# Selecting token rows over 128 partitions, and for one expert first in each layer's first group

## The reference, cut to what matters

```python
def hier_moe(x, wg, bg, we, be, w_gate_up, w_down):
    ...
    gsel = jnp.argmax(lg, axis=-1)                 # one of 4 groups per token
    ...
    topv, topi = lax.top_k(le_sel, MOE_TOP_K)      # 2 of the group's 4 experts
    wt = jax.nn.softmax(topv, axis=-1) * p_sel
    ...
    hu = jnp.einsum('td,edf->tef', xt, w_gate_up)  # 2048 -> 2*512 per expert
    hg, hv = jnp.split(hu, 2, axis=-1)
    act = jax.nn.silu(hg) * hv * gates[..., None].astype(x.dtype)
    out = jnp.einsum('tef,efd->td', act, w_down)   # 512 -> 2048
```

## Time and profile before

| | |
|---|---|
| median of 3 runs | 1442.11 us (1439.29 to 1442.18) |
| the profiled execution's own time | 1440.58 us |
| its span in the profile | 1438.5 us |
| TensorE matmul busy | 1354.8 us (94%) |
| TensorE weight load busy | 753.8 us (52%) |
| VectorE / ScalarE busy | 517.0 / 370.5 us |
| DMA | 489.03 MB, mean 340 GB/s |
| layer 0, first selection | 387.74 us into the span |
| layer 1, first selection | 941.09 us into the span |

### The profile page before, as it was taken

How to read it: one execution, slowest core, us unless ns; L and a number is a source line. 1 busy time by engine, 2 the same in 40 slices (tenths; PEclk the granted TensorE clock), 3 DMA queues, 4 the chain that set the end, 5 groups by cost and what they waited for, 6 DMA issues and landing times.

```text
span 1438.5 us, 20688 instructions
## 1 busy us (share of the span) xinstructions
PE 1354.8 (94%) x8992; PEld 753.8 (52%) x8992; DVE 517.0 (36%) x1068; ACT 370.5 (26%) x576; POOL 30.8 (2%) x40
## 2 busy tenths in 40 slices
PE   8999999999899999999899998899999899889985
PEld 8999999999643433343243226653243243224321
DVE  6877887743442122022004016633042013103303
ACT  5667666442310120030012004410021012002001
POOL 0000000000000000000000000000000000000000
PEclk9999999999899999999999999999999999999998
DMA  9776452944599999999999988689999999999993
GB/s 296 241 211 191 138 186 77 293 163 171 201 390 405 428 413 428 426 427 428 428 427 428 426 343 309 245 300 354 427 426 428 427 427 427 428 427 427 426 428 128
DMA packets 94759, 489.03 MB, mean 340 GB/s; under 512 B 8409, under 2 KB 64665, under 8 KB 67577
## 3 DMA queue, kind: packets, MB, share of 16 engines
q1 hardware_dynamic: 89536, 468.61, 82.0%
q10 hardware_dynamic: 2458, 10.27, 2.1%
q0 software_dynamic: 2672, 8.82, 1.6%
HBM read 481.95 MB, written 16.04 MB: 346 GB/s over the span
## 4 chain that ended last, share of the span: by engine, by line
PE 70%; DMA 25%; DVE 2%; ACT 1%; issue 1%; ACTq 0%; DVEq 0%; POOL 0%; SPq 0%; POOLq 0%
DMA ring<-in_moe_w_down 23%; PE ps L1325 19%; PE ps L1304 17%; PE ps L1071 5%; PE ps L1073 5%; PE ps L1072 5%; PE ps L1223 5%; PE ps L1159 2%; PE ps L1388 2%; PE ps L1160 2%; PE ps L1161 2%; PE ps L1247 1%; DMA ring<-in_lru_w_in 1%; ACT xtok L676 1%; DMA xtok<-x_rows,src_now 1%
## 5 line engine op out<-in xcount | busy, mean ns | idle before, releaser
L1304 PE MATMUL ps<-ring,xsel 128*64 128x512 f32 x2016 | 451.2, 596 | 30.1 <-DMA ring<-in_moe_w_gate_up 29.1
L1325 PE MATMUL ps<-ring,work 128*32 128x512 f32 x3072 | 342.9, 594 | 16.6 <-DMA ring<-in_moe_w_down 16.6
L1304 PEld LDWEIGHTS ps<-ring,xsel 128*64 128x64 f32 x2016 | 137.5, 137 | 316.7 <-issue 258.3
L1325 PEld LDWEIGHTS ps<-ring,work 128*32 128x32 f32 x3072 | 93.5, 110 | 234.2 <-issue 210.1
L1922 DVE SCALAR_TENSOR_TENSOR arena<-arena,ps 64x512 f32<-64x512 f32 x32 | 21.7, 678 | 480.8 <-ACT work L900 480.8
L1071 PE MATMUL ps<-operands,whi 128*128 128x288 f32 x512 | 153.2, 299 | 0.4 <-DVE ring_lo L1473 0.4
L1072 PE MATMUL ps<-ring_lo,whi 128*128 128x288 f32 x512 | 151.4, 296 | 0.0
L1073 PE MATMUL ps<-operands,ring_lo 128*128 128x288 f32 x512 | 151.4, 296 | 0.0
L1463 DVE TENSOR_TENSOR ring_lo<-ring,whi 128x1024 fp32r<-128x1024 f32 x96 | 115.8, 1220 | 58.5 <-ACT whi L692 58.2
L692 ACT ACTIVATE whi<-ring 128x1024 fp32r<-128x1024 f32 x96 | 100.5, 1057 | 127.7 <-PE ps L1073 71.7
L899 ACT ACTIVATE arena<-ps 64x512 f32<-64x512 f32 x32 | 18.8, 589 | 395.4 <-PE ps L1304 395.4
(11 more groups left out here) (368 smaller groups left out, 1168.2 us busy)
## 6 DMA issues: line engine op xcount, KB each, us to landing
ring<-in_moe_w_gate_up SPq DMA_DIRECT2D x126, 2048.0 KB, 21.3
ring<-in_moe_w_down SPq DMA_DIRECT2D x64, 2048.0 KB, 21.6
ring<-in_lru_w_in SPq DMA_DIRECT2D x15, 2048.0 KB, 10.4
ring<-in_lru_w_out SPq DMA_DIRECT2D x8, 2048.0 KB, 13.9
x_rows<-xtok ACTq DMA_DIRECT2D x4, 1024.0 KB, 3.9
xtok<-in_moe_w_gate_up SPq DMA_DIRECT2D x2, 2048.0 KB, 11.1
ring<-in_pool_w SPq DMA_DIRECT2D x4, 1024.0 KB, 12.5
xtok<-in_x_prompt SPq DMA_DIRECT2D x2, 1024.0 KB, 8.3
```

Source lines behind the costliest of these rows:

```text
L1304: last = mm(ps[half * ES:(half + 1) * ES, e % 2, :], xsel[:, k, e * ES:(e + 1) * ES], wt[:, half * 512:(half + 1) * 512], start=(k == 0), ...
L1325: last = mm(ps[rows:rows + QB, 2 + r, :], act[:, e % 2, f * W + slots0:f * W + slots0 + QB], wt[:, d * 512:(d + 1) * 512], start=start, st ...
```

## The change

In a layer's first window the selection is split. `select_rows(0, q)` now multiplies with the first 64 columns of `sel` alone (expert 0), at the same places as before. The other three experts' 192 columns follow in `select_rest(q)`, at parts 14, 16, ... 28 (`REST_AT`), each q in bank 2 or 3, scaled into `xsel` by ScalarE (`rest_rows`); expert 1's gates wait for them pair by pair. The blocks stay the stationary operand, so each of them is loaded twice. The gate-weighted copy of `sel` gets a place of its own (`first_sel`), since `sel` is needed until part 28, and the choice for the next window waits for the last rest selection.

In all windows the selection now runs over 128 partitions in place of 96: `row_block` takes all of `xtok[:, 0, :]`, and partitions 96 to 127 of `sel` are set to zero once. Some pairs of semaphores become one that counts on.

```diff
+REST_AT = {14 + 2 * q: q for q in range(PAIRS)}
...
+        first_sel = carve(work, 3584, NE, ES)
...
+                def rest_rows(parts):
+
+                    for q in parts:
+                        eng.wait_ge(rest_turned, PAIRS * l + q + 1)
+                        for b in range(2):
+                            k = 2 * q + b
+                            last = eng.activation(xsel[:, k, ES:NE * ES], ps[:, 2 + q % 2, b * 192:(b + 1) * 192], ACT.Identity,
+                                                  scale=affine_of[:, l, 0, k:k + 1], bias=affine_of[:, l, 1, k:k + 1])
+                        last.then_inc(rest_ready, 1)
+
...
+                    if first:
+                        rest_rows(range(0, 1))
                     eng.wait_ge(act_turned[l], w * (NE + 1) + 1)
...
+                        if first and e == 0:
+                            rest_rows(range(1, 4))
                         eng.wait_ge(act_turned[l], w * (NE + 1) + (e + 2))
                         eng.activation(act[:, e % 2, :], ps[:, 6 + e % 2, 0:KF * W], ACT.Copy).then_inc(act_ready[l], 1)
                         if e == 0 and first:
+                            rest_rows(range(4, 5))
                             eng.wait_ge(places_done, l + 1)
                             eng.activation(places_raw, ps[:, 5, RAW_AT:RAW_AT + WINS * W // 4], ACT.Copy).then_inc(places_out, 1)
+                            rest_rows(range(5, PAIRS))
...
                 for q in range(0, PAIRS, 2):
-                    even_rows(0, q)
+                    even_rows(0, q, 1)
...
+                def row_block(k):
+                    return xtok[:, 0, :].rearrange("s (c p j) -> s c j p", c=4, j=4)[:, k // 4, k % 4, :]
+
+                def select_rest(q):
+
+                    for b in range(2):
+                        last = mm(ps[:, 2 + q % 2, b * 192:(b + 1) * 192], row_block(2 * q + b),
+                                  sel[:, 1:NE, :].rearrange("p e j -> p (e j)"), start=True, stop=True)
+                    last.then_inc(rest_turned, 1)
+
-                def select_rows(w, q):
+                def select_rows(w, q, n=NE):
...
-                        last = mm(ps[:, 6 + q % 2, b * 256:(b + 1) * 256], XS.rearrange("s (c p j) -> s c j p", c=4, j=4)[:, k // 4, k % 4, :],
-                                  sel[0:W, :, :].rearrange("p e j -> p (e j)"), start=True, stop=True)
+                        last = mm(ps[:, 6 + q % 2, b * 256:b * 256 + n * ES], row_block(k),
+                                  sel[:, 0:n, :].rearrange("p e j -> p (e j)"), start=True, stop=True)
...
-                                select_rows(w, r)
+                                select_rows(w, r, 1 if first else NE)
+                        if first and i in REST_AT:
+                            select_rest(REST_AT[i])
...
+                            if first and e == 1 and k % 2 == 0:
+                                eng.wait_ge(rest_ready, PAIRS * l + k // 2 + 1)
...
-                    TT_(sel[0:W, :, :], sel[0:W, :, :], gslot[0:W, :].unsqueeze(2).to_broadcast([W, NE, ES]), ALU.mult)\
-                        .then_inc(sel_ready[l], 1)
+                    TT_((first_sel if first else sel)[0:W, :, :], sel[0:W, :, :],
+                        gslot[0:W, :].unsqueeze(2).to_broadcast([W, NE, ES]), ALU.mult).then_inc(sel_ready[l], 1)
...
                             eng.wait_ge(act_turned[l], w * (NE + 1) + 1)
+                            if first:
+                                eng.wait_ge(rest_turned, PAIRS * (l + 1))
                             choose(lk, slot_rank[0:W, bass.ds((w + 1) * NE, NE)])
...
+                if l == 0:
+                    V.memset(sel[W:128, :, :], 0.0)
                 one_hot(0, 1)
```

More of the change, by code:

```diff
@@ L346, in encoder_step @@
         sums_copied = sem("sums_copied")
-        stat_done = {i: sem(f"stat_done{i}") for i in (0, 2)}
-        var_ready = {i: sem(f"var_ready{i}") for i in (0, 2)}
-        std_ready = {i: sem(f"std_ready{i}") for i in (0, 2)}
+        stat_done = sem("stat_done")
+        var_ready = sem("var_ready")
+        std_ready = sem("std_ready")
         router_sums, router_ready, cols_ready = sem("router_sums"), sem("router_ready"), sem("cols_ready")
@@ L361, in encoder_step @@
         cnt_done = sem("cnt_done")
-        route_ready = [sem(f"route_ready{i}") for i in two]
+        route_ready = sem("route_ready")
         th_ready = [sem(f"th_ready{i}") for i in two]
@@ L399, in encoder_step @@
         pool_diff = sem("pool_diff")
+        rest_turned, rest_ready = sem("rest_turned"), sem("rest_ready")
         pext_ready, pext_free, scaled = sem("pext_ready"), sem("pext_free"), sem("scaled")
@@ L550, in _ @@
                     window_loads(l, w, w if l == 0 else w + extra, base)
-                eng.wait_ge(route_ready[l], 1)
+                eng.wait_ge(route_ready, l + 1)
                 n_win = eng.value_load(route_i[0:1, l, 0:1], min_val=NG, max_val=NG + MORE)
@@ L801, in layer_norm @@
                 squares(n, range(12, KD))
-                eng.wait_ge(stat_done[n], 1)
+                eng.wait_ge(stat_done, n + 1)
                 eng.activation(msq[:, 0:T], ps[:, 6, 0:T], ACT.Copy).then_inc(sums_copied, 1)
-                eng.wait_ge(var_ready[n], 1)
-                eng.activation(trstd, tvar, ACT.Sqrt).then_inc(std_ready[n], 1)
+                eng.wait_ge(var_ready, n // 2 + 1)
+                eng.activation(trstd, tvar, ACT.Sqrt).then_inc(std_ready, 1)
             def moe(l):
@@ L858, in even_rows @@
                         k = 2 * q + b
-                        last = eng.activation(xsel[:, k, :], ps[:, 6, b * 256:(b + 1) * 256], ACT.Identity,
+                        last = eng.activation(xsel[:, k, 0:n * ES], ps[:, 6, b * 256:b * 256 + n * ES], ACT.Identity,
                                               scale=affine_of[:, l, 0, k:k + 1], bias=affine_of[:, l, 1, k:k + 1])
@@ L1111, in sum_blocks @@
                 if r == KD // 4 - 1:
-                    last.then_inc(stat_done[n], 1)
+                    last.then_inc(stat_done, 1)
                 elif n == 2:
@@ L1238, in turn_spread @@
                     def turn_spread():
+                        weighted = first_sel if first else sel
                         for e in range(NE):
-                            last = nc.tensor.transpose(ps[0:ES, 7, e * W:(e + 1) * W], sel[0:W, e, :], ident[0:W, 0:W])
+                            last = nc.tensor.transpose(ps[0:ES, 7, e * W:(e + 1) * W], weighted[0:W, e, :], ident[0:W, 0:W])
                         last.then_inc(act_turned[l], 1)
@@ L1651, in layer_norm @@
                 V.tensor_copy(lgT[:, :], ps[:, 5, 0:T]).then_inc(lgT_ready, 1)
-                eng.wait_ge(stat_done[n], 2)
+                eng.wait_ge(stat_done, n + 2)
                 tmean, tmsq = ps[:, 7, 0:3], ps[:, 7, 3:6]
@@ L1656, in layer_norm @@
                 link(STT(tvar, tmsq, EPS, tvar, ALU.add, ALU.subtract))
-                TS_(tvar, tvar, EPS * 0.5, None, ALU.max).then_inc(var_ready[n], 1)
-                eng.wait_ge(std_ready[n], 1)
+                TS_(tvar, tvar, EPS * 0.5, None, ALU.max).then_inc(var_ready, 1)
+                eng.wait_ge(std_ready, n // 2 + 1)
                 link(V.reciprocal(trstd, trstd))
@@ L1794, in route @@
                     if x == MORE - 1:
-                        V.tensor_copy(route_i[0:1, l, :], route_f[0:1, :]).then_inc(route_ready[l], 1)
+                        V.tensor_copy(route_i[0:1, l, :], route_f[0:1, :]).then_inc(route_ready, 1)
                 base = C_MOE0 if l == 0 else C_MOE1
@@ L1825, in put_to, with odd_rows @@
                     ins.then_inc(dst_ready[l], 1)
-                def odd_rows(w, q):
+                def odd_rows(w, q, n=NE):
                     eng.wait_ge(rows_turned[l], w * PAIRS + (q + 1))
@@ L1963, in moe @@
                 for q in range(1, PAIRS, 2):
-                    odd_rows(0, q)
+                    odd_rows(0, q, 1)
                 for w in range(FLAT):
                     window(w, first=w == 0, ahead=w < FLAT - 1)
-                eng.wait_ge(route_ready[l], 1)
+                eng.wait_ge(route_ready, l + 1)
                 n_win = eng.value_load(route_i[0:1, l, 0:1], min_val=NG, max_val=NG + MORE)
```

6 lines of the change are left out of this document (3 added, 3 removed).

## The result

| | before | after |
|---|---|---|
| median, runs of one comparison | 1440.93 us (1439.29 to 1442.18, 4 runs) | 1454.72 us (1451.89 to 1459.77, 4 runs) |
| ratio, 95% interval | | 1.0097 [1.0076, 1.0117] |
| a later comparison | 1439.91 us (1438.18 to 1445.07, 9 runs) | 1451.26 us (1450.26 to 1454.84, 5 runs) |
| its ratio | | 1.0085 [1.0071, 1.0099] |

The change costs 13.8 us in the first comparison and 11.4 us in the second. The forecast was +10.5, at 1452.6.

The account below looks back on a forecast made before the run. In the expert stage TensorE or the down-weight stream was taken to bound, depending on place. Layer 0's 9.0 and layer 1's 1.5 made 10.5 us more, 1452.6 on a median of 1442.1; widened range 1444.5 to 1458.5.

Parts of the forecast that it names:

- the row of the router's loads: Router-row weight loads (line 1099), strided over 128 partitions, follow at 1.82 ns a column; nearest guide to the selections' 1.80.
- 0.23 us for a selection instruction after the change: Each selection instruction, with 64 or 192 columns, still takes 0.23 us; eight rest runs of 1.20 add 9.6 us.
- The start of the first gates: In a layer's first window, gates start 2.01 us behind the first selection in place of 2.17 by TensorE: gain 0.5.
- Breaks: Five newly broken runs of gates (parts 14, 18, 20, 26, 28) at 0.15 us each: 0.75 us.
- ScalarE costs nothing: ScalarE's eight pairs of 192 columns, 0.66 us each, fit between rest selections; if late, up to some 0.5 us.
- Layer 0: 9.0: Slots behind part 31 freed 9.4 us late against at most 1.4 us of stream slack: 8.0 to 9.4, taken as 9.0.
- Layer 1: 1.5: Layer 1's queue absorbs most of the 9.4 us delay; 1.5 us lost, between 0.5 and 4.
- slack 8.5 at 995.73 leaves 0.9: In layer 1 at 995.73, landing 16.1 less unqueued 7.6 gives 8.5 us of slack; of the 9.4 delay 0.9 remains.
- The second narrow place: Layer 1's chunk at 1072.99: slack 5.9 us against a remaining TensorE delay of 6.9, so 1.0 us.
- in part so: Rival: load hidden inside a run, but each run pays its first load; about 1442 us, chance 0.07.
- 96 partitions as the cause: Rival: 96 partitions slow the selections' load and 128 hide it; loads near 190 ns, 1437.7 us, chance 0.09.
- layer 1 pays in full: Rival: later broadcast loads meet the late chunks, or ScalarE is late; up to 9.4 + 9.4 = 18.8 us, 1461, chance 0.09.

Follow-up runs that it names:

- second trace: A second profiled execution of the same, unaltered changed kernel; 1451.21 us, without a clock fall in either layer's first window.
- one-layer version: Changed kernel with the selection split in layer 0's first window only, layer 1 as before; 1449.72 us, ratio 1.0072 to the kernel before.
- the two halves: Kernel before with selections over 128 partitions only, 1441.77 us; changed kernel with selections back on 96 partitions (the split only), 1454.62 us.
- first profile: First profiled execution of the changed kernel, the longest of its comparison; 1459.77 us, with a clock fall in layer 0's first window.

## Why the prediction was right

The price of an instruction, and with it the sign, came from the row of the router's loads; it held at every point.

- *0.23 us for a selection instruction after the change.* A run of eight with 64 columns lasts 2.01 us on the chain, forecast 2.01; a rest run of four 1.18, forecast 1.20, and one of them 1.01. All eight: 9.3, forecast 9.6.
- *The start of the first gates.* 2.50 us behind the first selection before (390.24 - 387.74), 2.03 now: 0.47 for a forecast of 0.5. The narrow evacuations do what they are for, and it is all they bring.
- *Breaks.* 9.09 measured in all, less 9.3, plus 0.47 and 3 x 0.16 leaves 0.7 for the five broken runs; forecast 0.75.
- *ScalarE costs nothing.* True for the gates. In layer 0 of the second trace PE waits for `xsel` once, 0.2 us, for a first pair; one weight load of the gates waits 0.3 us for a rest pair (line 863). The price was too low: a 192-column eviction took 507 ns, forecast 330, yet the pairs were ready. VectorE's late `choose` shows in no wait of PE's. Not true for layer 1's broadcast loads, as said below.
- *Layer 0: 9.0.* Measured 9.1 by the medians of the one-layer version (7.5 to 13.3), and 9.06 by the issue of layer 1's first loads. Its stream had no slack that lasted.
- *Layer 1: 1.5.* **This term was mis-sized.** It measured 2.3 to 3.3 us in the traces and 5.1 (3.6 to 7.6) by the medians; the gap between the two is open. The step that failed is "slack 8.5 at 995.73 leaves 0.9". Behind that place the stream was 1.8 us late, not 0.9, and it had stood still for 2.0 us. The slack was read as if all of the queue would wait for TensorE; but part of the work in it, the two broadcast loads, is issued by ScalarE and moved back too. The forecast named that ("the broadcasts also start some 10 us later"; measured 10.0) and gave it too little. It also put ScalarE at nothing without asking what stands behind the rest pairs in its program: the broadcasts do, and went out 2.24 us behind the tables in place of 0.04. That this order makes most of the 2.0 us is argued from the traces; no run moved the broadcasts ahead of the rest pairs. That they share the stream's rate is no difference: 273 GB/s beside them before (985 to 995.7 us), 260 in the second trace (997.7 to 1005.4). The second narrow place, forecast 1.0, added nothing clear: the stream was 2.5 us late ahead of it and about 2.6 behind it. So some 0.7 us were lost between the two places and some 0.6 behind both, where is open.
- *Clock.* The sum did not reckon with it. The first comparison's 13.8 lies 2.4 over the second's 11.4, with executions of one program between 1450 and 1460. That the falls make this difference is likely from the traces, but only three executions were traced.
- *Luck.* The forecast stood on a median before of 1442.1; the comparison found 1440.93. By the times it missed by 2.1 us (1454.72 against 1452.6), by the difference by 3.3 (13.8 against 10.5): the higher base hid a third of the miss.

With 9.1 and 3.3 the sum is 12.4, between the two comparisons. The rival sums redone: the 7.8 of "in part so" cannot be worked out from the terms that stand beside it; the others come out as they stand. The rivals: 96 partitions as the cause is refuted by the two halves; "in part so" by the 2.01 of a run; "layer 1 pays in full" had 9.4 for layer 1, above the 3.3 of the traces and the 7.6 that ends the medians' interval, but its reason, the broadcasts now later, is what layer 1 did pay for. Of the falsifiers that the prediction named, loads near 190 ns did not occur, nor a first window that is not longer; that the layers grew differently rests on the traces more than on the medians.

## What to carry to other kernels

When an operation is bound by its weight load, splitting it by moving columns pays the load twice and saves next to nothing; first look at how the stationary block lies in memory. Here a stride of four floats doubled the load, and a transposition that happened anyway undid it for free. Time from issue to landing above the unqueued time is slack only so far as the queue consists of the stream itself: ask which other transfers stand in it, who issues them, and what the change puts ahead of them in that engine's program. And where a stream runs at its full rate behind a delay, as in layer 0 here, the delay stays: ask of every step that is put ahead of a release what it does to the slot behind it.

## What the runs showed of the hardware that was not expected

- ScalarE's copy of 128x512 takes 1214 ns where consecutive results go 128 floats apart, and 779 where they follow each other: the kernel before with the fast loads bought this way took 1446.24 us, over the 1441.59 without them.
- A transposition with a reordered unit matrix as moving side costs no more: 306 ns a matmul against 312 with the plain one, in the kernels before with and without it.

```profile
L1008 PE MATMUL ps<-work,xT 128*128 128x128 f32 x64 | 9.2, 306 | 0.0
```

```profile
L1006 PE MATMUL ps<-ident,xT 128*128 128x128 f32 x64 | 9.5, 312 | 0.0
```

- The granted clock fell to 0.50 for about 10 us in the middle of a stretch where PE had been busy for 12 (390.4 to 402.4 us in the first profile), in some executions and not in others of one program. Shorter falls, about 3 us, began within 2.5 us of a first selection that had waited 1.65 to 3.27 us for its rows. Where TensorE is the bound a fall cost 1.3 to 4.6 us, as much as the effects studied here, so two single traces can mislead by that much.
